# A hybrid decoder block: two 128-channel outputs of a projection unit, computed one after the other or side by side

## The reference

```
z = rmsnorm(h) @ w_in                       # (272, 1024) @ (1024, 10240)
z_conv, z_q, z_k, z_v, z_g, z_gate = split(z)
a, b = split(z_conv);  u = conv31(a * sigmoid(b))      # depthwise, causal
y_conv = silu(layernorm(u)) @ w_conv_out + b_conv_out
y_ret  = (silu(z_g) * groupnorm(retention(rotary(z_q), rotary(z_k), z_v))) @ w_ret_out
h = h + (sigmoid(g_a) * y_conv + sigmoid(g_b) * y_ret) @ w_mix_out
h = h + moe(rmsnorm(h))                     # 32 experts, top 4, clamped SwiGLU
out = rmsnorm(h)[16:]
```

## Time and profile before

| what | value |
|---|---|
| three runs | 1322.84, 1320.12, 1321.0 us |
| median | 1321.0 us |
| profiled execution, first to last instruction | 1319.5 us |
| median over the profiled span | 1.5 us |
| TensorE busy | 1262.9 us (96%) |
| TensorE weight loads | 718.6 us (54%) |
| VectorE busy | 574.3 us (44%) |
| ScalarE busy | 293.4 us (22%) |

### The profile page before, as it was taken

How to read it: one execution, slowest core, us unless ns; L and a number is a source line. 1 busy time by engine, 2 the same in 40 slices (tenths; PEclk the granted TensorE clock), 3 DMA queues, 4 the chain that set the end, 5 groups by cost and what they waited for, 6 DMA issues and landing times.

```text
span 1319.5 us, 21209 instructions
## 1 busy us (share of the span) xinstructions
PE 1262.9 (96%) x8585; PEld 718.6 (54%) x8585; DVE 574.3 (44%) x1113; ACT 293.4 (22%) x508; POOL 14.3 (1%) x33
## 2 busy tenths in 40 slices
PE   8999999999999999998999999999999989999997
PEld 8999889999984344333333333333333333333332
DVE  5898899986646232222232222223222222232221
ACT  5453444445451111110110011001101110110101
POOL 1000000000000000000000000000000000000000
PEclk9999999999999999999999999999999999999999
DMA  9753454457698999999999999999999999999994
GB/s 324 229 166 127 129 175 141 138 182 227 256 371 318 413 431 432 432 432 429 430 432 432 434 432 430 430 433 432 433 432 430 430 433 432 433 432 424 428 427 197
DMA packets 77885, 467.48 MB, mean 354 GB/s; under 512 B 4375, under 2 KB 62279, under 8 KB 63287
## 3 DMA queue, kind: packets, MB, share of 16 engines
q1 hardware_dynamic: 77456, 466.79, 86.5%
q10 hardware_dynamic: 391, 0.16, 0.0%
HBM read 465.89 MB, written 1.05 MB: 354 GB/s over the span
## 4 chain that ended last, share of the span: by engine, by line
PE 62%; DMA 35%; DVE 1%; ACT 1%; issue 0%; ACTq 0%; DVEq 0%; SPq 0%
PE pb L802 18%; DMA work<-in_w_gate_up 9%; PE pb L829 9%; DMA work<-in_w_down 9%; DMA late_w<-in_w_gate_up 8%; PE pb L558 6%; PE pb L560 6%; PE pb L559 6%; DMA split_w<-in_w_down 4%; PE pb L859 2%; DMA split_w<-in_w_gate_up 2%; DMA late_w<-in_w_down 2%; PE pb L717 2%; PE pb L748 2%; PE pb L643 1%; PE pb L645 1%
## 5 line engine op out<-in xcount | busy, mean ns | idle before, releaser
L1648 DVE TENSOR_SCALAR work<-pb 64x512 f32<-64x512 f32 x64 | 43.7, 683 | 529.7 <-PE pb L809 529.7
L802 PE MATMUL pb<-work,ubuf 128*64 128x512 f32 x992 | 223.7, 604 | 19.7 <-DMA work<-in_w_gate_up 19.7
L558 PE MATMUL pb<-parts,whi 128*128 128x256 f32 (+1 forms) x640 | 184.8, 289 | 0.7 <-DVE parts L1210 0.7
L560 PE MATMUL pb<-parts,wlo 128*128 128x256 f32 (+1 forms) x640 | 182.4, 285 | 0.0
L559 PE MATMUL pb<-parts,whi 128*128 128x256 f32 (+1 forms) x640 | 182.2, 285 | 0.0
L802 PEld LDWEIGHTS pb<-work,ubuf 128*64 128x64 f32 x992 | 75.3, 139 | 154.9 <-issue 154.7
L1199 DVE TENSOR_TENSOR wlo<-work,whi 128x1024 fp32r<-128x1024 f32 x104 | 126.4, 1221 | 36.4 <-ACT whi L967 36.2
L967 ACT ACTIVATE whi<-work 128x1024 fp32r<-128x1024 f32 x104 | 109.3, 1058 | 121.9 <-PE pb L560 98.0
L802 PE MATMUL pb<-late_w,ubuf 128*64 128x512 f32 x576 | 127.5, 594 | 8.7 <-DMA late_w<-in_w_gate_up 8.7
L829 PE MATMUL pb<-work,ubuf 128*64 128x512 f32 x576 | 131.2, 597 | 2.8 <-DMA work<-in_w_down 1.3
L558 PEld LDWEIGHTS pb<-parts,whi 128*128 128x128 f32 x640 | 120.6, 188 | 3.6 <-issue 3.1
(11 more groups left out here) (246 smaller groups left out, 1312.3 us busy)
## 6 DMA issues: line engine op xcount, KB each, us to landing
work<-in_w_gate_up SPq DMA_DIRECT2D x28, 4096.0 KB, 30.8
split_w<-in_w_gate_up SPq DMA_DIRECT2D x14, 4096.0 KB, 30.1
late_w<-in_w_gate_up SPq DMA_DIRECT2D x13, 4096.0 KB, 30.8
work<-in_w_down SPq DMA_DIRECT2D x12, 4096.0 KB, 29.0
work<-in_w_in SPq DMA_DIRECT2D x40, 1024.0 KB, 5.2
late_w<-in_w_down SPq DMA_DIRECT2D x7, 4096.0 KB, 29.0
split_w<-in_w_down SPq DMA_DIRECT2D x7, 4096.0 KB, 29.0
work<-in_w_down SPq DMA_DIRECT2D x11, 2048.0 KB, 21.3
```

Of the source, the lines that this page charges most:

```text
L558: pe.matmul(o, wh, xh, start=first, stop=False)
L560: ins = pe.matmul(o, wl, xh, start=False, stop=last)
L802: ins = pe.matmul(pb[u * SLOTS:(u + 1) * SLOTS, bank, :], xT[:, 2 * i + k, :], w[:, k, u * HID:(u + 1) * HID], start=(i == 0 and k == 0), ...
L1648: dve.tensor_scalar(hg, pb[0:SLOTS, 4 + s, :], LIMIT, None, ALU.min).then_inc(min_rdy, 1)
```

## The change

Inside a unit the loop over the outputs j becomes the innermost one. For each block k and each of the three products, output 0 and output 1 now follow each other, so the bank changes with each product. The number of products, their operands and the order of the sums within one output stay. The increment of `full` for output 0 now comes after the last but one product of the unit. Nothing else is changed: the retention and convolution outputs keep the old order.

```diff
-                    for j in range(2):
-                        for k in range(KC // 2):
-                            wh, wl = (w[:, x, k * UNIT + j * P:k * UNIT + (j + 1) * P] for w in (whi, wlo))
-                            first, last = c == 0 and k == 0, c == 1 and k == KC // 2 - 1
-                            kc = c * KC // 2 + k
-                            o, xh, xl = pb[:, bank + j, 0:TALL - t0], nhi[:, kc, t0:TALL], nlo[:, kc, t0:TALL]
-                            pe.matmul(o, wh, xh, start=first, stop=False)
-                            pe.matmul(o, wh, xl, start=False, stop=False)
-                            ins = pe.matmul(o, wl, xh, start=False, stop=last)
-                        if c:
-                            ins.then_inc(full, 1)
+                    for k in range(KC // 2):
+                        first, last = c == 0 and k == 0, c == 1 and k == KC // 2 - 1
+                        kc = c * KC // 2 + k
+                        xh, xl = nhi[:, kc, t0:TALL], nlo[:, kc, t0:TALL]
+                        for w, of in ((whi, xh), (whi, xl), (wlo, xh)):
+                            for j in range(2):
+                                ins = pe.matmul(pb[:, bank + j, 0:TALL - t0], w[:, x, k * UNIT + j * P:k * UNIT + (j + 1) * P], of,
+                                                start=first and w is whi and of is xh, stop=last and w is wlo)
+                                if last and w is wlo:
+                                    ins.then_inc(full, 1)
                     if c == 0:
                         ins.then_inc(m_used, 1)
```

## The result

The changed kernel takes 1319.03 us (median of 20 runs, 1318.68 to 1321.24) against 1320.92 us before (20 runs): ratio 0.9984, 95% interval 0.9978 to 0.9990. That is 1.9 us less. It lies inside the range of the prediction and inside its 0.2%, but the interval leaves no room for "no change", which was the forecast. The profiled executions differ by 2.2 us: 1317.3 against 1319.5.

A forecast was written before the change was run, and what follows sets the result against it. TensorE was taken to bound the projections through its product spacing. Products 0, evacuation 0 and weights 0 left the span at 1319.5 us; with the runs' median 1.5 us above it, the forecast was 1321.0 us, range 1315 to 1326.

The forecast's parts named there:

- What bounds the kernel, and that a saving would reach the end: Projections: TensorE busy for all 44.00 us of a head, so product spacing or a new wait could change the time.
- The excess does not come from the bank: Projections: products take 9.3 or 10.2 ns above estimate, 18.7 us in all; a bank change is worth nothing within about 2 ns.
- Rival 1: Projections: staying in one bank does cost the excess, so the new order returns 17.5 us, giving 1304 us; chance 0.11.
- Products 0: Projections: the new order leaves the spacing of the 1920 products unchanged, 0 us.
- The eight distances at changes of bank: Two projection units: start distances where the bank changes total 0.98 us, against 978 ns by unit means, 900 without the excess.
- The bounds of ±2 ns: Projections: limits kept on the change per product, ±3.8 us in all, also covering tokens repeated by pairs.
- Rival 4: Projections: a small gain of 1.4 to 5 ns per product from position in a run, about 1315 us; chance 0.06.
- no measurable change: Whole kernel: likeliest case, time stays within 1318.4 to 1323.6 us; chance 0.72.
- The excess grows with the columns and is no fixed turn-around: Projections: 16 more columns cost 7.5 ns where one cycle per column is 6.7, unlike a fixed turn-around between instructions.
- Weights: Projections: losing the repeated weight load costs 0, since loads of lines 558 and 559 both take 188 ns.
- Later release of the first bank: Projection units: first bank's `full` comes 1.3 to 1.4 us later, conversion 0.2, at most 0.4 us later; cost 0.
- the cover of 4.0 us: Projections, second half of a head's first v unit: TensorE reaches VectorE's low part 4.0 us later, hiding the conversion's delay.

The follow-up runs named there:

- first experiment: Kernel before, still 12 products in a row to one bank, last two products of a block exchanged so no neighbours share weights: 126.1 (272 columns) and 118.2 ns (256).
- the four fixed blocks: Kernel before, each unit streaming only one token block; with 272 columns, blocks 0 to 3 gave 123.3, 125.4, 126.6 and 126.6 ns per product.
- staggered kernel: Changed kernel with the three high/low terms of the two outputs staggered, so no neighbours share weights: 1318.95 us, ratio 0.9981 to before.

## Why the prediction was wrong

- **What bounds the kernel, and that a saving would reach the end.** Right. The projections are TensorE's alone, and 2.0 us saved there are 2.05 us at the output projection and 1.9 us in the median.
- **The excess does not come from the bank.** Right, and shown from both sides: new order in one bank, 117.1 ns; old order in alternating banks, 118.2 and 126.1 ns. Rival 1 is out. The Trainium skill (Perfetto Trace Analysis, section Matmul Optimizations) asks that all eight PSUM banks be used, for instruction-level parallelism; alternating between two of them inside a unit brought nothing here.
- **Products 0.** This is the step that failed: "I take 0 for the new order". The measured term is -1.0 ns per product, -2.0 us. The eight distances at changes of bank were rightly read, but they only say what the bank costs. The same edit also changed how long a block of tokens is kept, from three products to six, and I left that without a price: "The moving operand is now repeated by pairs; no row shows a price for that, and the bounds above take it in." The bounds of ±2 ns did take it in; the sum and the chances did not follow them. Rival 4, a small gain of 1.4 to 5 ns, came nearest and had 0.06; its size begins above the measured one, and its reason, the position in a run to one bank, is not the one that the runs showed.
- **What a measurement can tell.** The prediction took 0.2% (2.6 us), from three runs that spread over 2.7 us, as the least change that could be told from none, and gave "no measurable change" 0.72. With 20 runs of each kernel the interval is 0.9978 to 0.9990, and 1.9 us stand clear of it.
- **The excess grows with the columns and is no fixed turn-around.** I used this only against the bank. It could have been read as a sign that something in the stream of tokens costs time. The runs show spacings from 123.3 to 126.7 ns (272) and from 113.3 to 119.9 ns (256) for different relative starts, so some part of the 9 to 10 ns above the estimates of 115.8 and 109.2 ns goes with the start. In no run did the excess vanish; the least, 113.3 ns in one unit, is 4.1 ns above 109.2. The two estimates are the prediction's own, from its float32 rows. The Trainium skill (TensorE: Matmul & The Clock Gate, section Back-to-back issue gap) has the same figures, N / 2.4 + 2.5 ns, as the warm gap of an isolated product, and says that they do not describe a stream of weight loads and products; the projections' 117.1 to 126.1 ns agree with that. So the excess over 109.2 and 115.8 is no measure of what an order could return.
- **Weights.** Right: no cost of repeated loads (first experiment).
- **Later release of the first bank.** Right in size (0.15 us for 0.2) and in effect (none). The Trainium skill (Perfetto Trace Analysis, section Matmuls) asks that independent groups of products rotate through banks so that the evacuation of one overlaps the products of the next; it does not decide here, because the cover of 4.0 us is long.

What stays open: the mean of the four fixed blocks is 125.5 ns with 272 columns, and the real loops lie on either side of it, 126.1 when the start changes every three products and 125.1 when it changes every six. That the order acts only where starts differ is shown by two pairs (blocks 0 and 4 in turn against block 0; the third head in both orders). Why a change of start costs or returns what it does is not, and its sign is not fixed: the new order saves 1.0 ns in the projections and costs 2.3 ns in the fourth head's quarter of the retention output. Nor is it known why block 3 with 256 columns ran at 113.3 and 113.8 ns in two units and at 117.8 in six of one execution, though the place behind other work may matter (not tested). The third head of the retention output has the same start, by the declared sizes, and runs at 117.8 ns.

## What to carry to other kernels

An edit of a loop's nesting changes every operand's sequence, not only the one it is meant for. List them all (bank, weights, streamed data) and give each its own price and its own bound before the sum is set to zero. When a gain is found, test the named cause from both sides, since the order and the bank could be separated here by two small edits. Compare data by where they start, not by their number in the loop: the two widths seemed to disagree only in the second way. And where products or loads run at the same rate for hundreds of microseconds, it can be worth trying where their buffers begin: 64 bytes were worth 3 us here, more than the change.

## What the runs showed of the hardware

- The spacing of float32r products depends on the start of the streamed data relative to the weights modulo 256 bytes: 113.5 to 119.9 ns for 256 columns, 123.3 to 126.7 ns for 272, with the least of both at one and the same start. If all products had it, 960 × (125.1 - 123.3) + 960 × (117.1 - 113.5) ns, about 5 us by estimate, would be to be had. Another stride of the token blocks alone does not give that, since the 256 columns start 64 bytes behind the 272 in the same block. With the start good for 256 columns in all products the projections took 265.4 us, against 267.3 in the changed kernel and 268.4 with the start good for 272. Storing the meta tokens so that both widths begin alike was not tried.
- The same loop can run at several steady spacings. The convolution output (192 products, changed by only one edit) ran at 121.1 ns in the profile of before, 120.1 in after, and in two executions of the same staggered kernel at 117.8 and 121.1 ns. That is 192 × 3.3 ns = 0.6 us between executions of one program.
- Expert loads into SBUF, with the DMA engines busy throughout, ran at 433 in place of 431 GB/s after a shift of the buffers by 64 bytes.
